# Router logits with the weights held and x streamed, expert choice behind the placing tables, first gate gathered in two rounded parts

## Chip, cores and metric

One core of a Trainium2 chip. The metric is the device time of one execution in microseconds (us); three runs of the kernel before give the median, and one more execution was profiled.

## What is computed

Two transformer stacks in a row on 256 tokens of width 1024, all in float32. In the first stack each of two layers ends in a mixture of experts, the part that the change touches (the reference, cut):

```python
def hier_moe(x, w_group, b_group, w_router, b_router, w_gate, w_up, w_down):
    t = x.reshape(-1, D)
    g_logits = (t @ w_group) + b_group                    # 4 groups
    g_prob = softmax(g_logits); g_idx = argmax(g_logits)
    g_w = g_prob at g_idx
    e_logits = ((t @ w_router).reshape(-1, 4, 4) + b_router) at g_idx
    top_w, top_i = top_k(softmax(e_logits), 2)
    top_w = top_w / sum(top_w)
    combine = onehot(g_idx) * within(top_i, top_w) * g_w  # 16 weights a token
    for e in range(16):
        y += combine[:, e] * ((silu(t @ w_gate[e]) * (t @ w_up[e])) @ w_down[e])
```

A token goes to one group of four experts. The second stack (dense feed-forward layers and a mixer) is left as it is.

## The kernel before, in words

The program of each engine is written out in order, and the engines meet at semaphores; nothing reorders it. TensorE works in rounded float32 (f32r). A value is split in two rounded parts, a high one (ScalarE, a rounding copy) and a low one (VectorE, value minus high part), and a product is three matmuls: high by high, high by low, low by high (L447 to L449). Weights come in units of 128 x 2048, 1 MB. SyncE loads unit i once TensorE has used unit i - 7, ScalarE rounds it (L404) once unit i - 4 is used, VectorE makes the low part (L416). In layer 0, GpSimd does that for one of the units.

The 256 tokens are two tiles (t = 0, 1). In a layer's mixture of experts the tokens are sorted by group: matrices of zeros and ones, `Pm`, put up to 128 tokens of a group in a row (`place_dve`, L1450), and TensorE gathers x by them, two groups at a time (`gather_two_pe`, L1261). The very first gate product, of expert 0, is computed for all 256 tokens while the routing is being worked out, and its result is gathered afterwards (`first_gate_pe`, L1330). All other experts work on gathered tokens, one tile of 128: gate, SiLU on ScalarE (L1527), times up and the token's weight on VectorE (L1535, the hidden block `hd`), turned by TensorE (L1544), down, and back to the tokens' places by `PT`, the turned `Pm` (`place_turn_pe`, L1457 and L1460).

The routing stage runs once a layer. TensorE (`route_pe`): logits of tile 0 (24 matmuls, x held as weights, 20 router columns streamed, L1296), gate unit 0 for tile 0, turning of x of tile 1 (L558), gate unit 1 for tile 0, logits of tile 1, gate unit 0 for tile 1, ranks of the tokens in their groups (L1308 to L1312), gate unit 1 for tile 1; then the gather of groups 0 and 1, the gather of the first gate's product, and the turning of `Pm` for group 0. Then come up units 2 and 3 (numbered from the first gate unit, 0), with the gather of groups 2 and 3 between them, gate units 4 and 5 of expert 1, with the turning of the first hidden block behind unit 4.

VectorE (`route_dve`): low parts of the turned x (L570) and of x itself (L1248), low part of unit 2, bias addition to the logits (L1386), choice of the group, choice of the two experts, placing tables, the tokens' weights `comb` (L1439), low parts of units 3 and 4, of the gathered x (L1279), tables of groups 2 and 3, units 5 and 6, the second gather, the hidden block. ScalarE (`route_act`): high parts of the turned x (L566), of units 2 and 3 (L404), of x (L1244), two exponentials, unit 4, SiLU of the first gate's two tiles (L1358), high parts of the gather (L1272). GpSimd scales X into Y (L1567) once `comb` is there.

## Time and profile before

| | us |
|---|---|
| median of 3 runs | 1907.75 (1907.04 to 1908.02) |
| profiled execution, its own time | 1906.78 |
| its span in the profile | 1905.0 |
| TensorE busy | 1860.3 |
| VectorE busy | 1295.7 |
| ScalarE busy | 1006.0 |

The span is what the rows below count in: us from its start. TensorE's mean granted clock is 0.986 of full speed. A matmul of an f32 tile without rounding shows as two records, one of f32r as one; in both the output's type is what the profile prints.

### The profile page before, as it was taken

Reading aid. Unit: us, or ns where it says so; the run is one execution under the profiler, and the core shown is the slowest. Engines: PE = TensorE matmul, PEld = TensorE weight load, DVE = VectorE, ACT = ScalarE, POOL = GpSimd, SP = SyncE. Lnnn points to the kernel's source line nnn. Section 1 sums busy time; section 2 is a strip of 40 time slices with the busy share of each in tenths; the row PEclk is TensorE's granted clock in tenths of the full one; section 3 lists DMA queues with packets and bytes.
Section 4 is the critical chain, followed back from the end, with each engine's and each line's share of the span. In section 5 each row is a group of like instructions: output and inputs, shape, how many; then the busy total and the mean of one; then the engine's idle time right before and its main releaser. Section 6 shows DMA issues by size and latency. Waiting matters only on the chain.

```text
span 1905.0 us, 21839 instructions
## 1 busy us (share of the span) xinstructions
PE 1860.3 (98%) x9118; PEld 1549.1 (81%) x9118; DVE 1295.7 (68%) x1313; ACT 1006.0 (53%) x1069; POOL 123.5 (6%) x105
## 2 busy tenths in 40 slices
PE   7999999998999999998999999999999999999998
PEld 6788888887978888886888887888888888778886
DVE  4569999997778898997555657655464545676544
ACT  6446777774646777774443364444344424635431
POOL 1021000001011000000000300100010003020000
PEclk9999999999999999998999999999999998999999
DMA  9447999996435999996555642655565556336551
GB/s 339 152 147 249 358 370 359 357 361 201 145 129 196 370 356 358 357 372 213 179 196 172 214 138 88 202 194 169 188 221 178 177 175 206 120 131 201 184 178 59
DMA packets 220170, 426.56 MB, mean 224 GB/s; under 512 B 7560, under 2 KB 28304, under 8 KB 220064
## 3 DMA queue, kind: packets, MB, share of 16 engines
q1 hardware_dynamic: 214256, 406.91, 62.0%
q0 software_dynamic: 5808, 18.17, 3.0%
q8 instruction: 74, 1.21, 0.3%
q14 instruction: 32, 0.26, 0.0%
HBM read 423.99 MB, written 1.06 MB: 223 GB/s over the span
## 4 chain that ended last, share of the span: by engine, by line
PE 92%; DVE 4%; ACT 2%; DMA 1%; issue 1%; POOL 0%; DVEq 0%; SPq 0%
PE ps L447 26%; PE ps L449 26%; PE ps L448 26%; DVE Wlo L416 2%; PE ps L558 2%; PE ps L2429 1%; PE ps L2399 1%; PE ps L2335 1%; ACT Whi L404 1%; PE ps L1544 1%; PE ps L538 1%; PE ps L537 1%; PE ps L536 1%; PE ps L2415 1%; PE ps L1937 1%
## 5 line engine op out<-in xcount | busy, mean ns | idle before, releaser
L416 DVE TENSOR_TENSOR Wlo<-raw,Whi 128x2048 fp32r<-128x2048 f32 (+2 forms) x387 | 868.3, 2247 | 445.1 <-ACT Whi L404 444.4
L404 ACT ACTIVATE Whi<-raw 128x2048 fp32r<-128x2048 f32 (+2 forms) x393 | 736.3, 1877 | 480.6 <-PE ps L449 476.1
L447 PE MATMUL ps<-Whi,XTh 128*128 128x512 f32 (+2 forms) x1504 | 579.3, 385 | 14.2 <-DVE Wlo L416 8.1
L449 PE MATMUL ps<-Whi,XTl 128*128 128x512 f32 (+2 forms) x1504 | 569.7, 379 | 0.0
L448 PE MATMUL ps<-Wlo,XTh 128*128 128x512 f32 (+2 forms) x1504 | 569.4, 379 | 0.0
L447 PEld LDWEIGHTS ps<-Whi,XTh 128*128 128x128 f32 x1504 | 287.6, 191 | 70.7 <-DVE Wlo L416 9.6
L449 PEld LDWEIGHTS ps<-Whi,XTl 128*128 128x128 f32 x1504 | 286.8, 191 | 52.5
L448 PEld LDWEIGHTS ps<-Wlo,XTh 128*128 128x128 f32 x1504 | 287.4, 191 | 49.8 <-issue 0.5
L447 PE MATMUL ps<-Whi,hTh 128*128 128x512 f32 x352 | 137.7, 391 | 0.0
L449 PE MATMUL ps<-Whi,hTl 128*128 128x512 f32 x352 | 137.1, 389 | 0.0
L448 PE MATMUL ps<-Wlo,hTh 128*128 128x512 f32 x352 | 137.0, 389 | 0.0
L447 PE MATMUL ps<-Whi,mo_hTh 128*128 128x512 f32 x256 | 100.9, 394 | 0.0
L447 PE MATMUL ps<-Whi,XGh 128*128 128x512 f32 x256 | 100.8, 394 | 0.0
L664 POOL TENSOR_TENSOR rs<-rs,cst 128x1 f32<-128x1 f32 x20 | 30.6, 1528 | 1073.7 <-DVE rs L656 1073.7
L449 PE MATMUL ps<-Whi,mo_hTl 128*128 128x512 f32 x256 | 99.8, 390 | 0.0
L449 PE MATMUL ps<-Whi,XGl 128*128 128x512 f32 x256 | 99.8, 390 | 0.0
L448 PE MATMUL ps<-Wlo,mo_hTh 128*128 128x512 f32 x256 | 99.7, 389 | 0.0
L448 PE MATMUL ps<-Wlo,XGh 128*128 128x512 f32 x256 | 99.7, 389 | 0.0
L449 PEld LDWEIGHTS ps<-Whi,hTl 128*128 128x128 f32 x352 | 66.1, 188 | 13.9
L447 PEld LDWEIGHTS ps<-Whi,hTh 128*128 128x128 f32 x352 | 66.1, 188 | 13.4
L448 PEld LDWEIGHTS ps<-Wlo,hTh 128*128 128x128 f32 x352 | 66.1, 188 | 13.3
L566 ACT ACTIVATE XTh<-ps 128x512 fp32r<-128x512 f32 (+1 forms) x44 | 23.6, 577 | 97.8 <-PE ps L558 97.6
(327 smaller groups left out, 1867.5 us busy)
## 6 DMA issues: line engine op xcount, KB each, us to landing
raw<-in_moe_w_gate SPq DMA_DIRECT2D x64, 1024.0 KB, 5.4
raw<-in_moe_w_up SPq DMA_DIRECT2D x64, 1024.0 KB, 5.5
raw<-in_moe_w_down SPq DMA_DIRECT2D x64, 1024.0 KB, 5.7
raw<-in_ffn_gate SPq DMA_DIRECT2D x44, 1024.0 KB, 5.1
raw<-in_ffn_up SPq DMA_DIRECT2D x44, 1024.0 KB, 5.1
raw<-in_ffn_down SPq DMA_DIRECT2D x40, 1024.0 KB, 5.0
raw<-in_w_in SPq DMA_DIRECT2D x18, 1024.0 KB, 6.4
raw<-in_a_w_in SPq DMA_DIRECT2D x10, 1024.0 KB, 12.3
```

Of the source, the lines that this page charges most:

```text
L404: act.activation(Whi[:, i % NS, 0:m * n], raw[:, i % NR, 0:m * n], ACT.Copy).then_inc(w_rounded, tick(w_rounded, "rounded", i))
L416: dve.tensor_tensor(Wlo[:, i % NR, 0:m * n], raw[:, i % NR, 0:m * n], h.bitcast(f32), ALU.subtract).then_inc(w_rest, tick(w_rest, "rest", i))
L447: pe.matmul(o, xh(k, t), h[:, q, :], start=k == first, stop=False)
L448: pe.matmul(o, xh(k, t), l[:, q, :], start=False, stop=False)
L449: x = pe.matmul(o, xl(k, t), h[:, q, :], start=False, stop=k == end)
L536: pe.matmul(o, h[:, q, c], XTh[:, q, :], start=q == 0, stop=False)
L537: pe.matmul(o, h[:, q, c], XTl[:, q, :], start=False, stop=False)
L538: x = pe.matmul(o, l[:, q, c], XTh[:, q, :], start=False, stop=q == m - 1)
L558: x = pe.transpose(PS[b][:, q * 128:(q + 1) * 128], blk, cst[:, C_ID:C_ID + 128])
L566: act.activation(dst, src, ACT.Copy).then_inc(act_done, tick(act_done, "hi", *name))
L664: pool.tensor_tensor(rs[:, t, 1:2], rs[:, t, 0:1], cst[:, C_ONE + 1:C_ONE + 2], ALU.pow).then_inc(pool_done, tick(pool_done, "root", v, t))
L1544: x = pe.transpose(PS[b][:, q * 128:(q + 1) * 128], hd[:, u, q * 128:(q + 1) * 128], cst[:, C_ID:C_ID + 128])
```

## The change

The router's weights become the held operand: high and low part side by side, 40 columns (`rws`), and x's high and low parts of a tile are streamed, 128 columns a matmul, 16 matmuls a tile. The result stands turned, 40 x 256. VectorE copies it out of PSUM (`lgT`), and two small full-precision matmuls turn it back and add the two parts by a constant table (`C_SUM`), in the middle of gate unit 0 of tile 1.

TensorE does both gate units of tile 0 and the turning of x ahead of all logits. The product of the first gate is no longer put through SiLU before its gather: it is split in a high and a low part (`fgh`, `fgl`), gathered by four rounded matmuls, and SiLU comes behind. The placing tables are made ahead of the choice of the two experts. The turning of `Pm` for group 0 stands behind up unit 2. The low part of unit 2 moves from ahead of the bias addition to behind the gather's low parts.

```diff
@@ -17,7 +17,8 @@
 C_ALL1 = 1352
 C_IOTA = 1480
 C_OWN = 1608
-C_N = 1616
+C_SUM = 1616
+C_N = 1640
 
 
 def constant_table():
@@ -48,6 +49,7 @@
         t[:, C_CADD + 16 * tt:C_CADD + 16 * tt + 16] = np.where(see, 0.0, NEG)
         t[:, C_CMUL + 16 * tt:C_CMUL + 16 * tt + 16] = see
     t[:, C_OWN:C_OWN + 8] = i[:, None] // 16 == np.arange(8)[None, :]
+    t[:40, C_SUM:C_SUM + 20] = i[:40, None] % 20 == np.arange(20)[None, :]
     t[:, C_I4:C_I4 + 4] = 4 - np.arange(4)[None, :]
     t[:, C_ONE] = 1.0
     t[:, C_ONE + 1] = -0.5
@@ -209,8 +211,7 @@
     lam = small("df_lam", [128, 4, 64])
     gs = small("df_gs", [128, 1])
     rw = small("rw", [128, 8, 20])
-    rwh = small("rwh", [128, 8, 20], f32r)
-    rwl = small("rwl", [128, 8, 20], f32r)
+    rws = small("rws", [128, 8, 2, 20], f32r)
     rb = small("rb", [128, 20])
     lg = small("lg", [128, 2, 20])
     comb = small("comb", [128, 2, 16])
@@ -1221,11 +1222,11 @@
 
     def router_act(act, l):
         act.wait_ge(*on("rw", l))
-        act.activation(rwh[:, :, :], rw[:, :, :], ACT.Copy).then_inc(act_done, tick(act_done, "router_hi", l))
+        act.activation(rws[:, :, 0, :], rw[:, :, :], ACT.Copy).then_inc(act_done, tick(act_done, "router_hi", l))
 
     def router_dve(dve, l):
         dve.wait_ge(*on("router_hi", l))
-        dve.tensor_tensor(rwl[:, :, :], rw[:, :, :], rwh[:, :, :].bitcast(f32), ALU.subtract).then_inc(
+        dve.tensor_tensor(rws[:, :, 1, :], rw[:, :, :], rws[:, :, 0, :].bitcast(f32), ALU.subtract).then_inc(
             dve_done, tick(dve_done, "router", l))
 
 
@@ -1281,25 +1282,34 @@
             free(dve_done, *n)
 
 
+
+
+    lgT = at_("lgT", [40, 256], f32, big_o + 32768)
+
     def route_pe(pe, l, v):
-        b = bank(pe, "logits", l, hold=True)
+        b = bank(pe, "logitsT", l, hold=True)
         name, ready = ("gate", l, 0, 0), x_ready(v)
         js = jobs[name]
         bs = [bank(pe, name, t, hold=True) for t in range(2)]
 
         def logits(t):
-            for g in range(2):
-                pe.wait_ge(*on("lo", "xT", v, t, g))
-            first = True
             for k in range(8):
-                for a, w in ((XTh, rwh), (XTh, rwl), (XTl, rwh)):
-                    x = pe.matmul(PS[b][:, 32 * t:32 * t + 20], a[:, k, t * 128:(t + 1) * 128], w[:, k, :],
-                                  start=first, stop=(k == 7 and a is XTl))
-                    first = False
+                ready(pe, k, t)
+                for a in (XTh, XTl):
+                    x = pe.matmul(PS[b][0:40, t * 128:(t + 1) * 128], rws[:, k].rearrange("p a n -> p (a n)"),
+                                  a[:, k, t * 128:(t + 1) * 128], start=k == 0 and a is XTh, stop=k == 7 and a is XTl)
+            x.then_inc(pe_done, tick(pe_done, "logitsT", l))
+
+        def logits_turn():
+            b = bank(pe, "logits", l)
+            pe.wait_ge(*on("lgT", l))
+            for t in range(2):
+                x = pe.matmul(PS[b][:, 32 * t:32 * t + 20], lgT[:, t * 128:(t + 1) * 128], cst[0:40, C_SUM:C_SUM + 20],
+                              start=True, stop=True)
             x.then_inc(pe_done, tick(pe_done, "logits_mm", l))
 
         def gate(u, t):
-            use_unit(pe, js[u], t, bs[t], xt_h, xt_l, ready, 0, 7)
+            use_unit(pe, js[u], t, bs[t], xt_h, xt_l, ready, 0, 7, 2 if (u, t) == (0, 1) else None, logits_turn)
 
         def ranks():
             b = bank(pe, "ranks", l)
@@ -1312,10 +1322,10 @@
             pe.matmul(PS[b][:, 8:12], a1, oh[:, 1, :], start=False, stop=True).then_inc(
                 pe_done, tick(pe_done, "ranks", l))
         pe.wait_ge(*on("router", l))
+        gate(0, 0)
+        gate(1, 0)
+        second_pe(pe, v)
         logits(0)
-        gate(0, 0)
-        second_pe(pe, v)
-        gate(1, 0)
         logits(1)
         held.discard(b)
         gate(0, 1)
@@ -1323,16 +1333,33 @@
         gate(1, 1)
         held.difference_update(bs)
 
+
+    fgh = at_("fgh", [128, 2, 512], f32r, sh_o)
+    fgl = at_("fgl", [128, 2, 512], f32r, sh_o + 4096)
+
+    def first_half_act(act, l, t):
+        name = ("gate", l, 0, 0)
+        act.wait_ge(*product(name, t))
+        act.activation(fgh[:, t, :], PS[where[name, t]][:, :], ACT.Copy).then_inc(act_done, tick(act_done, "gate_hi", l, t))
+
+    def first_half_dve(dve, l, t):
+        name = ("gate", l, 0, 0)
+        dve.wait_ge(*on("gate_hi", l, t))
+        dve.tensor_tensor(fgl[:, t, :], PS[where[name, t]][:, :], fgh[:, t, :].bitcast(f32), ALU.subtract).then_inc(
+            dve_done, tick(dve_done, "gate_lo", l, t))
+        free(dve_done, name, t)
+
     def first_gate_pe(pe, P, l):
         b = bank(pe, "first", l)
         for t in range(2):
-            pe.wait_ge(*on("silu", l, t))
-            x = pe.matmul(PS[b][:, :], Pm[:, t, 0, :].bitcast(f32), sg[:, t, :], start=t == 0, stop=t == 1)
+            pe.wait_ge(*on("gate_lo", l, t))
+            for a in (fgh, fgl):
+                x = pe.matmul(PS[b][:, :], Pm[:, t, 0, :], a[:, t, :], start=t == 0 and a is fgh, stop=t == 1 and a is fgl)
         x.then_inc(pe_done, tick(pe_done, "first", l))
 
     def first_gate_act(act, P, l):
         act.wait_ge(*on("first", l))
-        act.activation(sg[:, 0, :], PS[where["first", l]][:, :], ACT.Copy).then_inc(
+        act.activation(sg[:, 0, :], PS[where["first", l]][:, :], ACT.Silu).then_inc(
             act_done, tick(act_done, P.name, "sg", 0, 0))
         free(act_done, "first", l)
 
@@ -1348,16 +1375,14 @@
         x_split_act(act, l, v, 0)
         second_act(act, v)
         x_split_act(act, l, v, 1)
+        first_half_act(act, l, 0)
         act.wait_ge(*on("group_gap", l))
         act.activation(ex, ex, ACT.Exp).then_inc(act_done, tick(act_done, "group_exp", l))
+        first_half_act(act, l, 1)
+        gather_two_act(act, l, 0)
         act.wait_ge(*on("top_gap", l))
         act.activation(g_(5), g_(5), ACT.Exp).then_inc(act_done, tick(act_done, "top_exp", l))
         round_units(act, js[0] + NS)
-        for t in range(2):
-            act.wait_ge(*product(name, t))
-            act.activation(sg[:, t, :], PS[where[name, t]][:, :], ACT.Silu).then_inc(
-                act_done, tick(act_done, "silu", l, t))
-            free(act_done, name, t)
 
     def first_max(dve, dst, src, tmp, mx, *name):
         dve.wait_ge(*own(dve_done))
@@ -1374,13 +1399,15 @@
             dve_done, tick(dve_done, *name))
 
     def route_dve(dve, l, v):
+        x_split_dve(dve, l, 0)
         x_turn_dve(dve, v, 1)
-        for t in range(2):
-            x_split_dve(dve, l, t)
-        rest_units(dve, last_unit(v) + NS - 1)
+        first_half_dve(dve, l, 0)
         tmp, ex, el, o1, o2 = (o4[:, i, :, :] for i in range(5))
         L4 = lg[:, :, 0:4]
         OH = oh[:, :, :]
+        dve.wait_ge(*on("logitsT", l))
+        dve.tensor_copy(lgT[:, :], PS[where["logitsT", l]][0:40, 0:256]).then_inc(dve_done, tick(dve_done, "lgT", l))
+        free(dve_done, "logitsT", l)
         dve.wait_ge(*on("logits_mm", l))
         dve.wait_ge(*on("rw", l))
         dve.tensor_tensor(lg[:, :, :],
@@ -1389,6 +1416,21 @@
         free(dve_done, "logits", l)
         first_max(dve, OH, L4, tmp, g_(0), "oh", l)
         dve.tensor_tensor(ex, L4, gb_(0), ALU.subtract).then_inc(dve_done, tick(dve_done, "group_gap", l))
+        x_split_dve(dve, l, 1)
+        dve.wait_ge(*on("ranks", l))
+        dve.tensor_copy(rank[:, :, :], PS[where[("ranks", l)]][:, 0:12].rearrange("p (t g) -> p t g", g=4)
+                        ).then_inc(dve_done, tick(dve_done))
+        free(dve_done, "ranks", l)
+        dve.wait_ge(*own(dve_done))
+        dve.tensor_scalar(gm[:, :, :], rank[:, 0:2, :], float(CAP), None, ALU.is_lt).then_inc(dve_done, tick(dve_done))
+        dve.wait_ge(*own(dve_done))
+        dve.tensor_tensor(gm[:, :, :], gm[:, :, :], oh[:, :, :], ALU.mult).then_inc(dve_done, tick(dve_done))
+        dve.wait_ge(*own(dve_done))
+        for g in range(2):
+            place_dve(dve, MAIN[l], g, rank, gm)
+        dve.tensor_scalar(rest[:, :, :], rank[:, 0:2, :], float(CAP), None, ALU.subtract).then_inc(
+            dve_done, tick(dve_done))
+        dve.tensor_reduce(fmax[:, :], rank[0:1, 2, :], AX.X, ALU.max).then_inc(dve_done, tick(dve_done))
 
         pr = bc(lg[:, 0, 4:5], (20, 2), (4, 4), (1, 4))
         pk = bc(pk_[:, 0, 0:1], (16, 2), (4, 4), (1, 4))
@@ -1406,21 +1448,9 @@
         first_max(dve, o2, ex, tmp, g_(4))
         dve.wait_ge(*own(dve_done))
         dve.tensor_tensor(g_(5), g_(4), g_(3), ALU.subtract).then_inc(dve_done, tick(dve_done, "top_gap", l))
-
-        dve.wait_ge(*on("ranks", l))
...
+        first_half_dve(dve, l, 1)
+        gather_two_dve(dve, l, 0)
+        rest_units(dve, jobs["up", l, 0, 0][0])
 
         dve.wait_ge(*on("top_exp", l))
         dve.scalar_tensor_tensor(g_(6), g_(5), 1.0, g_(2), ALU.add, ALU.mult).then_inc(dve_done, tick(dve_done))
@@ -1438,7 +1468,6 @@
         ohb = bc(oh[:, 0, 0:1], (4, 2), (1, 4), (0, 4))
         dve.tensor_tensor(bc(comb[:, 0, 0:1], (16, 2), (4, 4), (1, 4)), o1b, ohb, ALU.mult).then_inc(
             dve_done, tick(dve_done, "comb", l))
-        rest_units(dve, jobs["gate", l, 0, 0][0] + NS)
 
 
     class Path:
@@ -1574,7 +1603,6 @@
         route_pe(pe, l, v)
         gather_two_pe(pe, l, 0)
         first_gate_pe(pe, P, l)
-        place_turn_pe(pe, P, l, 0)
         for g in range(4):
             par = g % 2
             ps = slice(par * 128, par * 128 + 128)
@@ -1607,6 +1635,7 @@
                                 scatter_halves_pe(pe, P, g - 1, t, hf)
                 for z in job_pe(pe, ("up", l, g, j), xh, xl, ready, 1):
                     if z + g + j == 0:
+                        place_turn_pe(pe, P, l, 0)
                         gather_two_pe(pe, l, 1)
             for hf in range(2):
                 for z in job_pe(pe, ("down", l, g, hf), hh, hl, h_ready, 1, hold=int((g, hf) == (3, 1))):
@@ -1628,9 +1657,7 @@
         P = MAIN[l]
         place = act.soon()
         route_act(act, l, v)
-        gather_two_act(act, l, 0)
         first_gate_act(act, P, l)
-        place_turn_act(act, P, 0)
         round_units(act, jobs["gate", l, 0, 0][1] + NS)
         for g in range(4):
             for j in range(4):
@@ -1643,6 +1670,7 @@
                         h_turn_act(act, P, g, j - 1, mTh[:, 4 * j - 4:4 * j, :])
                 for z in job_act(act, ("up", l, g, j), None, 1):
                     if z + g + j == 0:
+                        place_turn_act(act, P, 0)
                         gather_two_act(act, l, 1)
             for hf in range(2):
                 name = ("down", l, g, hf)
@@ -1668,7 +1696,6 @@
         P = MAIN[l]
         place = dve.soon()
         route_dve(dve, l, v)
-        gather_two_dve(dve, l, 0)
         for g in range(2, 4):
             place_dve(dve, P, g, rank, gm)
         rest_units(dve, jobs["gate", l, 0, 0][1] + NS)
```

The order of VectorE's instructions shows two places. First, from the turned x of tile 1 to the bias addition, layer 0, before (names end in h and l for high and low parts):

```order
L672 SCALAR_TENSOR_TENSOR X<-Y,rs,gb 128x512 x2
L83 BRANCH_PREFETCH_HINT
L570 TENSOR_TENSOR XTl<-ps,XTh 128x4x128 x2
L1248 TENSOR_TENSOR Xnl<-X,Xnh 128x1024 x2
L416 TENSOR_TENSOR Wlo<-raw,Whi 128x2048
L1386 TENSOR_TENSOR lg<-ps,rb 128x40
```

and with the change:

```order
L673 SCALAR_TENSOR_TENSOR X<-Y,rs,gb 128x512 x2
L85 BRANCH_PREFETCH_HINT
L1249 TENSOR_TENSOR Xnl<-X,Xnh 128x1024
L571 TENSOR_TENSOR XTl<-ps,XTh 128x4x128 x2
L1348 TENSOR_TENSOR fgl<-ps,fgh 128x512
L1409 COPY lgT<-ps 40x256
L1413 TENSOR_TENSOR lg<-ps,rb 128x40
```

The second half of x's low part and unit 2's low part have left; the first gate's low part and the logits' copy have come.

Second, VectorE from the tokens' weights to the first hidden block, before:

```order
L1439 TENSOR_TENSOR comb<-o_79,oh 128x32
L416 TENSOR_TENSOR Wlo<-raw,Whi 128x2048 x2
L1279 TENSOR_TENSOR XTl<-ps,XTh 128x512 x4
L1450 TENSOR_SCALAR Pm<-cst,rank,gm 128x128 x4
L416 TENSOR_TENSOR Wlo<-raw,Whi 128x2048 x2
L1279 TENSOR_TENSOR XGl<-ps,XGh 128x512 x4
L1535 SCALAR_TENSOR_TENSOR hd<-sg,cwt,ps 128x512
```

and with the change, from the gather's low parts on (the rows left out are the tokens' weights, small ones):

```order
L1280 TENSOR_TENSOR XTl<-ps,XTh 128x512 x4
L417 TENSOR_TENSOR Wlo<-raw,Whi 128x2048
...
L1469 TENSOR_TENSOR comb<-o_78,oh 128x32
L1479 TENSOR_SCALAR Pm<-cst,rank,gm 128x128 x4
L417 TENSOR_TENSOR Wlo<-raw,Whi 128x2048 x4
L1280 TENSOR_TENSOR XGl<-ps,XGh 128x512 x4
L1564 SCALAR_TENSOR_TENSOR hd<-sg,cwt,ps 128x512
```

The gather's low parts have moved ahead of `comb`, with one unit behind them, and four units in a row stand between `comb` and the second gather.

ScalarE in the same stage, before:

```order
L566 ACTIVATE XTh<-ps 128x4x128 x2
L404 ACTIVATE Whi<-raw 128x2048 x2
L1244 ACTIVATE Xnh<-X 128x1024
L1352 ACT_TABLE_LOAD
L1352 ACTIVATE o_79<-o_79 128x8
L1354 ACTIVATE gx<-gx 128x2
```

and with the change:

```order
L567 ACTIVATE XTh<-ps 128x4x128 x2
L405 ACTIVATE Whi<-raw 128x2048 x2
L1245 ACTIVATE Xnh<-X 128x1024
L1343 ACTIVATE fgh<-ps 128x512
L1380 ACT_TABLE_LOAD
L1380 ACTIVATE o_78<-o_78 128x8
```

The first gate's high part, on which VectorE's `fgl` waits, stands behind two units and x.

## Rows read from the trace of the kernel before

**Rows 1.** The page's busy times: us, share of the span, instructions.
```profile
PE 1860.3 (98%) x9118; PEld 1549.1 (81%) x9118; DVE 1295.7 (68%) x1313; ACT 1006.0 (53%) x1069; POOL 123.5 (6%) x105
```

**Rows 2.** Busy us by stage and engine, then granted clock, DMA share, GB/s.
```profile
128.60:133.00 4.40, 4.40 (x14) 3.44 (x14) 2.37 (x3) 0.00 (x0) 2.51 (x3) 0.61 0.45 174
139.20:142.90 3.70, 3.70 (x11) 2.90 (x11) 3.57 (x4) 1.35 (x2) 0.00 (x0) 0.55 0.00 0
240.00:280.00 40.00, 40.00 (x183) 32.93 (x182) 36.06 (x22) 29.93 (x21) 0.00 (x0) 1.00 1.02 366
435.40:439.00 3.60, 3.33 (x7) 1.80 (x8) 2.72 (x5) 0.05 (x1) 0.89 (x1) 0.66 1.10 351
560.70:563.10 2.40, 0.25 (x3) 0.01 (x1) 1.88 (x3) 1.88 (x3) 0.00 (x0) 1.00 1.01 361
```

**Rows 3.** TensorE in order of time, layer 0: start, us, engine, line, operation.
```profile
125.91 0.24 PE L1296 MATMUL ps<-rwh,XTh 128*128 128x20 f32 x1
...
133.01 1.03 PE L558 MATMUL ps<-cst,X 128*128 128x128 f32 x8
...
136.63 0.17 PE L1296 MATMUL ps<-rwh,XTh 128*128 128x20 f32 x1
...
139.22 0.49 PE L447 MATMUL ps<-Whi,XTh 128*128 128x512 f32 x1
...
143.89 0.39 PE L1308 MATMUL ps<-oh,cst 128*128 128x4 f32 x2
...
145.03 0.48 PE L447 MATMUL ps<-Whi,XTh 128*128 128x512 f32 x1
...
148.53 0.38 PE L1261 MATMUL ps<-Pm,Xnh 128*128 128x256 f32 x1 [0.50 <-DVE Pm L1450]
...
152.46 1.88 PE L1330 MATMUL ps<-sg,Pm 128*128 128x512 f32 x4
...
162.27 0.40 PE L447 MATMUL ps<-Whi,XTh 128*128 128x512 f32 x1
...
167.75 0.60 PE L1544 MATMUL ps<-cst,hd 128*128 128x128 f32 x4
...
435.43 0.47 PE L1510 MATMUL ps<-Ygh,PT 128*128 128x512 f32 x1 [3.70 <-DVE Ygl L1698]
```

**Rows 4.** VectorE in order of time, the same stretch.
```profile
130.09 1.42 DVE L672 SCALAR_TENSOR_TENSOR X<-Y,rs,gb 128x512 f32<-128x512 f32 x2 [0.53 <-POOL rs L664]
...
139.30 1.23 DVE L1248 TENSOR_TENSOR Xnl<-X,Xnh 128x1024 fp32r<-128x1024 f32 x1 [2.60 <-ACT Xnh L1244]
...
140.44 2.28 DVE L416 TENSOR_TENSOR Wlo<-raw,Whi 128x2048 fp32r<-128x2048 f32 x1
...
142.65 0.19 DVE L1386 TENSOR_TENSOR lg<-ps,rb 128x40 f32<-128x40 f32 x1
...
149.52 5.33 DVE L416 TENSOR_TENSOR Wlo<-raw,Whi 128x2048 fp32r<-128x2048 f32 x2
...
162.86 2.48 DVE L1279 TENSOR_TENSOR XGl<-ps,XGh 128x512 fp32r<-128x512 f32 x4
...
165.25 0.73 DVE L1535 SCALAR_TENSOR_TENSOR hd<-sg,cwt,ps 128x512 f32<-128x512 f32 x1
```

**Rows 5.** ScalarE in order of time, the same stretch.
```profile
133.64 1.09 ACT L566 ACTIVATE XTh<-ps 128x512 fp32r<-128x512 f32 x2 [8.66 <-PE ps L558]
...
138.21 1.05 ACT L1244 ACTIVATE Xnh<-X 128x1024 fp32r<-128x1024 f32 x1
```

**Rows 6.** TensorE in order of time, full-precision matmuls of 128 columns.
```profile
1140.32 1.05 PE L2433 MATMUL ps<-mx_wcT,mx_vcz 128*128 128x128 f32 x8
```

**Rows 7.** GpSimd in order of time, the scaling of X.
```profile
149.70 7.78 POOL L1567 TENSOR_SCALAR Y<-X 128x1024 f32<-128x1024 f32 x2 [16.77 <-DVE comb L1439]
```

**Rows 8.** Tile lg: ns min/median/max, first and last start us.
```profile
L1386 DVE TENSOR_TENSOR lg<-ps,rb x2: 191/192/193, 142.6 to 579.9; 128x40 f32<-128x40 f32 x2
```

**Rows 9.** Line 518: weight loads of 16 columns, ns.
```profile
L518 PEld LDWEIGHTS ps<-XTh,Whi x8: 93/94/95, 21.3 to 23.8; 128*16 128x16 f32 x8
```

13 lines of the change are left out of this document (removed).

## The prediction

> **What bounds the kernel now.** I read the page's busy shares first. TensorE is busy for 1860.3 of 1905.0 us, VectorE for 68% [rows 1]: time is won where TensorE idles, repeats or runs slowly, and lost where another engine makes it wait. Then the busy times by stage: inside the experts' loop TensorE works 40.00 of 40.00 us at the full clock [rows 2], so whatever the routing stage before it gains or loses stays to the end. Third, TensorE in order of time through the routing stage of layer 0, from the first router matmul at 125.91 us to the first turn of a hidden block at 167.75 us [rows 3]. Layer 1 repeats it 437.2 us later: the addition of the router's bias starts at 142.6 and 579.9 us [rows 8]. The change touches only this stage, so I work out one pass, and take it twice.
>
> The stage costs more than its arithmetic. One token tile's logits are 24 matmuls of 20 moving columns: 2.59 us (136.63 to 139.22) [rows 3]. Behind each such block the granted clock falls: 0.61 over 128.6 to 133.0 us, 0.55 over 139.2 to 142.9 us, so most of these stretches ran at 1.2 GHz instead of 2.4 [rows 2]. A weight unit takes 2.74 us at the full clock (162.27 to 167.75 is two); the one from 139.22 took until 143.89, 4.67 us [rows 3]. Last I read VectorE and ScalarE over the same stretch [rows 4, 5], since the change reorders them more than it does TensorE.
>
> **The change, part by part.** A unit is 1 MB of weights; gate units 0 and 1 are the first expert's, up units 2 and 3 follow, then 4, 5 and 6.
>
> *TensorE up to the logits.* New order: both gate units of tile 0, the turning of tile 1, both logits, gate unit 0 of tile 1. From 125.91 us: two units, 5.5 us, to 131.4; the turn 0.8 us (133.01 to 136.63 is 3.6 with a unit in it) [rows 3], to 132.2; X of tile 1 is complete at 130.09 + 1.42 = 131.5 us [rows 4]. The logits are now 2 x 16 matmuls, 40 weight columns, 128 moving columns of rounded type. No row has that form. Lower bound: 0.11 us each, the pace of the present ones (2.59 / 24), or less, since the weights are narrower. Upper bound: 0.22 us, two records of 128 full-precision columns (8 records in 1.05 us; with the last one's own end of about 0.25 taken off they start 0.11 apart, two to a matmul) [rows 6]. I take 0.22, the only row with 128 moving columns, and keep the lower one as a rival. So 7.0 us, to 139.2. Half a unit, 1.4 us, to 140.6. Two small full-precision matmuls turn the logits back: four records at the pace of the rank matmuls (10 in 143.89 to 145.03), 0.45 us. The bias addition can start at 141.2 us; before, 142.65 [rows 4]. Lead: 1.4 us. With 7.0 us of wide matmuls for 5.2 us of narrow ones I expect no fall of the clock here, which is worth some 1.7 us per block (4.67 or, from the first, about 4.4 against 2.74).
>
> The Trainium skill, page "TensorE: Matmul & The Clock Gate", section "LDWEIGHTS (loading the stationary operand)", has the load time go with the number of columns; the trace agrees in direction, 94 ns for 16 columns [rows 9] against a mean of 170 over all loads (1549.1 / 9118) [rows 1]. With its 56 ns of section "Back-to-back issue gap" for 128 columns the 32 matmuls would take an estimated 1.8 us; that falls in the first rival.
>
> *A new wait ahead of the logits' copy.* VectorE now computes the low part of the first gate's tile 0 before it copies the logits out. For that it needs ScalarE's high part, which stands behind two roundings and the rounding of X. From the first turned copy to the end of that X rounding is 133.64 to 139.27, 5.6 us [rows 5]. With the turn at 131.4 ScalarE starts at 132.0 (0.63 behind it, as now) and is through at 137.7; the high part, a 128x512 copy of about 0.55 us, at 138.2; VectorE's low part, 0.62 (a quarter of 2.48 [rows 4]), at 138.9; the copy of the logits about 0.4 more, 139.3. TensorE wants it at 140.6: hidden by 1.3 us if a logits matmul costs 0.22, a stall if it costs 0.11 or less.
>
> *VectorE from the bias addition to the first hidden block.* Before: 142.65 to 165.98 us, 23.3 us [rows 4]. To this the change adds: the low part of unit 2, 2.2 us, which stood ahead of the addition (140.44 to 142.65); the low part of X's tile 1, 1.1 us (139.30 to 140.44); tile 1 of the first gate's low part, 0.6 us. Both the logits and the hidden block now enclose them. Three units instead of two are subtracted while GpSimd scales X for 7.78 us [rows 7]; the two there took 5.33, so 2.67 each, against 2.28 for one alone [rows 4]: 0.4 us. And two short waits, for the ranks and for the last quarter of the gather, about 0.5 us. Sum 4.8 us. The hidden block ends at 141.2 + 23.3 + 4.8 = 169.3 us. It ended at 165.98, and TensorE took it at 167.75: it was 1.6 us early, not counting 0.2 us from the end to the start of the next. Now it is taken at 169.5.
>
> *TensorE behind the logits.* 141.05 + 1.4 + ranks 1.1 + unit 2.8 = 146.4: the gather starts 2.1 us before today's 148.53, and its matrices are ready. Gather 3.9 (148.53 to 152.46) [rows 3], to 150.3. The first gate's gather, four rounded matmuls of 0.23 instead of full precision, about 0.95 for 1.7 us, to 151.3. Then up unit 2 needs its low part, which VectorE now makes behind the gather's: at about 154.2. TensorE idles 3 us. Up unit 2.8, placing turn 0.7 (moved here), second gather 3.8, two units 5.5: 167.0. The turn of the hidden block waits until 169.5, 2.5 us. Before: 167.75. **Net: 1.7 us later, per layer, 3.4 us in all.** What TensorE itself gained, 3.6 us per layer, goes into two waits for VectorE. Behind it VectorE catches up, since it is busy for 36.06 of 40 us in the loop [rows 2], and the DMA queue is paced by TensorE's use of buffers, so it shifts as a whole.
>
> The sum stands against the profiled execution, 1906.78 us: 1910.2. The median of the three runs is 1.0 us above it, 1907.75: **1911.2 us**, 0.18% more. Some 0.2%, 3.8 us, is what a measurement of this kernel can tell from no change.
>
> **The rivals.**
> *The logits matmuls cost 0.11 us or less* (20 in 100). TensorE then wants the copy at 137.2 or earlier, and stalls to 139.3: the bias addition starts at 140.1, 1.1 us earlier than forecast. The rest is VectorE's chain: +0.6 us per layer, 1909.0 us. For it: the present rounded matmuls show no sign of more than one pass.
> *VectorE's chain does not decide* (16 in 100). If its 4.8 us were 1 us or less, or the work between overlapped more than I see, TensorE alone sets the pace: 151.3 + 2.8 + 0.7 + 3.8 + 5.5 = 164.1 against 167.75, 3.6 us gained per layer: 1900.5 us. Half of it would give 1904. Against it: the order of VectorE's instructions is fixed, and all of them stand before the hidden block.
> *The clock falls behind the new waits* (14 in 100, the side of slower). TensorE idles 3 us before up unit 2 and 2.5 us before the hidden block's turn. A fall behind the first is covered by the second wait; a fall behind the second costs 1.7 us per layer, as measured behind the logits. 1914.6 us, or 1912.9 if it comes in one layer. It decides once the second wait is long enough to lower the clock. For it: behind a present wait, in which TensorE did nothing until 435.43 us, the granted clock is 0.66 over the next 3.6 us [rows 2, 3]. Against it: that wait lasts 3.70 us; over the one at 560.7 to 563.1 us, 2.4 us and thus the length of the second, the clock stays at 1.00 [rows 2]. [...]
> *The change does little of what it says* (5 in 100): the clock still falls in the stage, since the two small matmuls and the ranks remain narrow. It would cost up to 1.7 us per layer before the gather, half covered by the wait for up unit 2: 1912 to 1913.
>
> **How the numbers follow.** The forecast itself has 45 in 100, with a range of its own from 1909.5 to 1913. The range of all runs from 1904.5, which takes in half of the gain without the waits, to 1914.6. Slower by over 0.2% (above 1911.6): the clock's rival, the last one, and a third of the forecast: 0.34. Faster by over 0.2% (below 1903.9): most of the second rival: 0.15. The rest, 0.51, is within 0.2%.
>
> **What would show it.** Right, if TensorE's first hidden turn begins about 1.7 us later than today, with a wait for VectorE of some 2.5 us before it, and one of some 3 us before the first up unit. A logits matmul should start every 0.22 us, and the granted clock between 126 and 143 us be full. The gather should start near 146.4 us, and the logits' copy wait for nothing but the logits. Wrong, if the hidden block is taken without a wait, or if VectorE's stretch from the bias addition to it is nearer 23 than 28 us.

## The result and the profile after

The changed kernel takes **1915.97 us** (median of 19 runs, 1908.96 to 1922.55) against 1908.15 us (19 runs, 1906.66 to 1912.01) for the kernel before: ratio 1.0038, 95% interval 1.0030 to 1.0047, slower by 0.38%. I had forecast 1911.2 us with a range to 1914.6, so the direction of the likeliest number was right and its size was not: some 8 us were lost, not 3.4, and the median lies above the range.

The page's busy times of the changed kernel, the row that answers to [rows 1]:

```profile
PE 1857.3 (97%) x9094; PEld 1546.3 (81%) x9094; DVE 1298.5 (68%) x1319; ACT 1006.7 (53%) x1069; POOL 134.1 (7%) x105
```

TensorE works 3.0 us less than before and the span is 9.3 us longer (1914.3 against 1905.0), so it idles 57.0 us where it idled 44.7. The clock is slower as well: the mean granted clock is 0.984, before 0.986. The stretches at half speed in the trace add up to 61.3 us of the span, against 51.9, and 9.4 us more of them cost up to 4.7 us. So up to half of the loss is the clock, which the forecast had booked as a gain, and the rest is waits that outweigh the work saved. Busy time by stage (PE, PEld, DVE, ACT, POOL, then granted clock, DMA share, GB/s), the routing stage of layer 0 in the first three rows, a stretch of the experts, and the routing stage of layer 1 in the rest:

```profile
125.90:138.90 13.00, 10.23 (x71) 8.32 (x70) 8.10 (x13) 6.82 (x7) 5.23 (x4) 1.00 0.57 197
139.60:143.00 3.40, 3.40 (x12) 2.78 (x11) 2.23 (x8) 0.21 (x1) 0.00 (x0) 0.50 0.00 0
143.00:168.90 25.90, 21.69 (x131) 18.77 (x131) 23.95 (x51) 16.35 (x19) 13.09 (x2) 1.00 0.48 162
240.00:280.00 40.00, 40.00 (x184) 33.08 (x183) 36.31 (x22) 30.24 (x22) 0.00 (x0) 1.00 1.03 368
566.30:569.70 3.40, 3.40 (x10) 2.66 (x9) 3.11 (x6) 0.00 (x0) 1.30 (x1) 0.50 0.33 129
579.90:590.10 10.20, 9.18 (x28) 7.85 (x29) 6.18 (x27) 0.21 (x1) 0.00 (x0) 0.50 0.32 104
```

The experts' stretch reads as before [rows 2]: TensorE busy throughout at the full clock. Most of the loss is in the routing stage. Up to 138.9 us layer 0 no longer has the first slow stretch of [rows 2]. The second one is still there, at half clock (1.2 GHz) over 139.6 to 143.0 us, and in layer 1 the clock is at half over 579.9 to 590.1 us, three times as long, and once more at the stage's opening.

TensorE in order of time, layer 0, the answer to [rows 3]:

```profile
132.41 0.22 PE L1299 MATMUL ps<-XTh,rws 128*40 128x128 f32 x1
...
133.20 0.22 PE L1299 MATMUL ps<-XTl,rws 128*40 128x128 f32 x1
...
134.49 0.22 PE L1299 MATMUL ps<-XTl,rws 128*40 128x128 f32 x1
139.28 0.78 PE L1307 MATMUL ps<-cst,lgT 40*128 40x20 f32 x4 [3.13 <-DVE lgT L1409]
142.71 0.42 PE L1318 MATMUL ps<-oh,cst 128*128 128x4 f32 x2
146.72 0.28 PE L1262 MATMUL ps<-Pm,Xnh 128*128 128x256 f32 x1
150.57 0.40 PE L1357 MATMUL ps<-fgh,Pm 128*128 128x512 f32 x1
154.34 0.50 PE L448 MATMUL ps<-Whi,XTh 128*128 128x512 f32 x1 [2.68 <-DVE Wlo L417]
168.95 0.66 PE L1573 MATMUL ps<-cst,hd 128*128 128x128 f32 x4 [1.58 <-DVE hd L1564]
```

Three waits for VectorE stand there where [rows 3] has one of 0.50: 3.13 us for the turned logits' copy, 2.68 for the low part of up unit 2, 1.58 for the hidden block. The first one I had called hidden. The logits are the reason: from the third to the sixteenth matmul of tile 0, 132.41 to 133.20 us, 13 steps take 0.79 us, **0.061 us a step**, where I had taken 0.22. TensorE therefore stands at the copy well ahead of VectorE. (The Trainium skill, page "TensorE: Matmul & The Clock Gate", section "Wait — 56ns, not 53.3ns?", gives 55.6 ns a step for 128 columns at the full clock; this trace comes near it, at 61 for rounded float32.)

VectorE and ScalarE in the same stretch, the answers to [rows 4, 5]:

```profile
132.69 1.29 DVE L571 TENSOR_TENSOR XTl<-ps,XTh 128x512 fp32r<-128x512 f32 x2
138.21 0.69 DVE L1348 TENSOR_TENSOR fgl<-ps,fgh 128x512 fp32r<-128x512 f32 x1 [4.23 <-ACT fgh L1343]
138.82 0.41 DVE L1409 COPY lgT<-ps 40x256 f32<-40x256 f32 x1
140.09 0.20 DVE L1413 TENSOR_TENSOR lg<-ps,rb 128x40 f32<-128x40 f32 x1 [0.87 <-PE ps L1307]
144.06 0.17 DVE L1421 COPY rank<-ps 128x12 f32<-128x12 f32 x1 [1.57 <-PE ps L1322]
...
155.21 1.83 DVE L1479 TENSOR_SCALAR Pm<-cst,rank,gm 128x128 fp32r<-128x128 f32 x4
156.96 8.88 DVE L417 TENSOR_TENSOR Wlo<-raw,Whi 128x2048 fp32r<-128x2048 f32 x4
...
168.16 0.73 DVE L1564 SCALAR_TENSOR_TENSOR hd<-sg,cwt,ps 128x512 f32<-128x512 f32 x1
```

```profile
133.03 3.72 ACT L405 ACTIVATE Whi<-raw 128x2048 fp32r<-128x2048 f32 x2
136.64 1.05 ACT L1245 ACTIVATE Xnh<-X 128x1024 fp32r<-128x1024 f32 x1
137.58 0.60 ACT L1343 ACTIVATE fgh<-ps 128x512 fp32r<-128x512 f32 x1
```

This is the chain of the new wait. The copy of the logits (`lgT`) stands behind `fgl` on VectorE; `fgl` needs `fgh`; `fgh` stands behind two weight units and x on ScalarE. VectorE itself does nothing for 4.23 us ahead of it, with the logits lying in PSUM (the memory that TensorE writes its results to) from about 134.7 us on.

Layer 1 repeats the pattern, and there it costs far more:

```profile
565.90 0.51 PE L448 MATMUL ps<-Whi,XTh 128*128 128x512 f32 x1 [2.17 <-DVE Y L680]
...
580.92 1.04 PE L1307 MATMUL ps<-cst,lgT 40*128 40x20 f32 x4 [3.14 <-DVE lgT L1409]
...
584.62 0.42 PE L1318 MATMUL ps<-oh,cst 128*128 128x4 f32 x2
```

From the wait's end to the ranks is 3.43 us in layer 0 (139.28 to 142.71) and 3.70 us here; but the clock stays at half for another 5.5 us behind the ranks' start. The first row above shows a wait of 2.17 us for `Y`, at the start of layer 1's stage. In a table, between points that both traces have (waits are those in front of the point):

| stretch | before | after | difference |
|---|---|---|---|
| layer 0, first gate work to first hidden turn | 125.9 to 167.75 | 125.9 to 168.95 | +1.20 |
| to the wait for Ygl at the end of its experts | to 435.43 | to 437.35 | +0.72 |
| to the start of layer 1's routing stage | to 563.12 | to 565.90 | +0.86 |
| layer 1, to its first hidden turn | to 605.01 | to 613.29 | **+5.50** |
| to the wait for Ygl at the end of its experts | to 871.95 | to 880.23 | 0.00 |
| the rest | to 1905.0 | to 1914.3 | +1.02 |

The same instructions cost 1.20 us in one layer and 5.50 in the other. The work and the waits are alike (3.13 and 3.14, 2.68 and 2.68, 1.58 and 1.62 us); what differs is 10.2 us at half clock against 3.4 in the wait's wake. 6.8 us more at half speed are up to 3.4 us of time, and the stage's opening has 3.4 us of it as well (566.3 to 569.7), up to 1.7 us more.

The table's other rows hold 2.60 us that lie outside the two stages. There the clock is at half over 436.6 to 443.4 us and over 880.3 to 894.0 us, 6.8 and 13.7 us long, where the trace of before has 3.4 us (from 436.5) and 10.2 us (from 873.5). That is up to 1.7 us more each time, in places that the change does not touch.

### The profile page after: what moved, and what is told of

Its sections match the earlier page's. It is cut to its first block, busy times and chain, and to the rows that moved or that the text cites. A ratio compares the mean times of both kernels' runs of the same rounds, so it can differ in the third digit from the quotient of the medians.

```text
span 1914.3 us, 21795 instructions
## 1 busy us (share of the span) xinstructions
PE 1857.3 (97%) x9094; PEld 1546.3 (81%) x9094; DVE 1298.5 (68%) x1319; ACT 1006.7 (53%) x1069; POOL 134.1 (7%) x105
## 4 chain that ended last, share of the span: by engine, by line
PE 92%; DVE 4%; ACT 2%; DMA 1%; issue 1%; POOL 0%; DVEq 0%; SPq 0%
PE ps L448 26%; PE ps L450 26%; PE ps L449 26%; DVE Wlo L417 2%; PE ps L559 2%; PE ps L2456 1%; PE ps L2426 1%; ACT Whi L405 1%; PE ps L2362 1%; PE ps L1573 1%; PE ps L539 1%; PE ps L538 1%; PE ps L537 1%; PE ps L2442 1%; PE ps L1964 1%
```

## The experiments

Two theories at first. **The clock**: the long wait for the turned logits makes the granted clock fall, and that fall, not the wait, is the main loss. **The chain**: VectorE's longer way to the hidden block is the loss, as in my forecast, and the clock only accompanies it. The kernels ran in three groups, each beside runs of the kernel before on the same chip (medians 1907.8, 1907.2 and 1908.1 us). The changed kernel itself was measured beside other runs of the kernel before (1908.15 us), so between it and an experiment the ratios, each to its own runs of before, are safer than the medians.

**1. The logits' copy ahead of the first gate's low part** (takes the wait away).

```diff
     def route_dve(dve, l, v):
         x_split_dve(dve, l, 0)
         x_turn_dve(dve, v, 1)
-        first_half_dve(dve, l, 0)
...
         dve.tensor_tensor(ex, L4, gb_(0), ALU.subtract).then_inc(dve_done, tick(dve_done, "group_gap", l))
+        first_half_dve(dve, l, 0)
         x_split_dve(dve, l, 1)
```

> The changed kernel, with VectorE's copy of the turned logits (lgT) ahead of the first gate's low part instead of behind it. In the changed kernel TensorE waits 3.13 us for that copy (layer 0), and the granted clock falls right behind. Theory (the loss is the wait for the copy with the fall of the clock behind it, plus VectorE's longer chain): the 3.1 us wait goes, no fall of the clock near the ranks, the bias addition starts near 136.6 us instead of 140.09, and the turn of the first hidden block begins near 165.5 us instead of 168.95; time about 3 us under the kernel before, so some 10 us under the change. Rival (only VectorE's chain from the bias addition to the hidden block counts, the clock does not): 3.5 us per layer gained against the change's layer 0, so the same in layer 0, but the two layers gain equally. Rival (the loss sits elsewhere, behind the routing stage): less than 2 us gained.

Measured 1904.91 us (1902.51 to 1911.78), ratio to before 0.9984 (0.9975 to 0.9993): against the changed kernel's 1.0038 some 10 us won by moving one instruction of 0.69 us. TensorE in layer 0:

```profile
135.76 0.62 PE L1307 MATMUL ps<-cst,lgT 40*128 40x20 f32 x4
...
149.89 0.79 PE L448 MATMUL ps<-Whi,XTh 128*128 128x512 f32 x1 [2.68 <-DVE Wlo L417]
165.53 0.60 PE L1573 MATMUL ps<-cst,hd 128*128 128x128 f32 x4
```

The logits are turned 3.5 us earlier, without a wait, and the hidden block is taken at 165.53, 3.4 us earlier. Now the wait for unit 2 is the long one, and the clock is at half for 6.8 us from 149.2 us on, 0.7 us before that wait ends. Layer 1's stage (561.94 to 602.54 us) takes 40.60 us instead of 47.39, so the layers do not gain equally, as the rival without the clock wanted. But the mean granted clock is hardly better than the changed kernel's, 0.985 against 0.984, worth up to 1.7 us: most of this gain is the wait that is gone and all that now starts earlier.

**2. The wait filled** (keeps it, takes TensorE's idleness away): 14 matmuls of 512 columns, whose result is overwritten.

```diff
         def logits_turn():
             b = bank(pe, "logits", l)
+            for q in range(14):
+                pe.matmul(PS[b][:, :], XTh[:, q % 8, 128:256], halves(js[0])[0][:, q % 4, :], start=True, stop=True)
             pe.wait_ge(*on("lgT", l))
```

> The changed kernel with 14 matmuls of 512 columns put in TensorE's wait for the turned logits; they write a bank that is written anew afterwards and change no result. The wait itself stays as it is, TensorE is only busy in it. Theory (the clock falls because of this wait and costs several us, more in layer 1): the half-clock stretch behind it vanishes in both layers, the time falls from about 1916 to 1909 to 1911 us, and the spread between runs shrinks to that of the kernel before. Rival (the clock's part is small, the loss is the chain of waits): within 1 us of the change or slower by it, since 3 us of work were added to a wait of 3.1.

Measured 1906.37 us (1905.58 to 1909.97), ratio 0.9994 (0.9985 to 1.0003), 9.6 us below the changed kernel by the medians and 8.4 by the ratios, more than the expected 5 to 7.

```profile
135.84 3.36 PE L1306 MATMUL ps<-Whi,XTh 128*128 128x512 f32 x14
139.13 0.62 PE L1309 MATMUL ps<-cst,lgT 40*128 40x20 f32 x4
```

```profile
139.60:143.00 3.40, 3.40 (x22) 2.93 (x22) 2.74 (x11) 0.21 (x1) 0.00 (x0) 1.00 0.13 23
577.00:590.00 13.00, 10.32 (x65) 8.99 (x65) 11.84 (x42) 6.40 (x10) 0.00 (x0) 0.99 0.50 163
152.80:156.20 3.40, 3.40 (x9) 2.62 (x10) 3.30 (x11) 2.46 (x3) 2.49 (x1) 0.50 0.01 2
589.70:593.10 3.40, 3.35 (x8) 2.71 (x9) 3.26 (x12) 2.66 (x3) 2.31 (x1) 0.50 0.01 2
```

So the clock is a large part of the loss. The turned logits come hardly earlier than in the changed kernel (139.13 against 139.28), the order of VectorE's work is untouched, TensorE has 3.2 us more work per layer, and the kernel is 0.4 to 0.5% faster. The clock is at 1.00 and 0.99 where it was at 0.50. The first hidden turns are at 167.27 and 604.36 us, against 168.95 and 613.29: layer 1's stage, from 562.73 us, takes 41.63 us instead of 47.39.

It does not isolate one fall, though. In each layer 3.4 us at half clock have moved to the wait for unit 2 (the last two rows), where the changed kernel's layer 0 has 1.00. The mean granted clock is 0.988, and the stretches at half speed add up to 44.9 us against the changed kernel's 61.3. Nearly 7 of these 16 us are the stretches behind the logits (3.4 and 10.2 us) less the two new ones; the others are gone from 436, 566 and 880 us, which the filling does not touch. Why those change is open.

**3. Half the filling.**

```diff
-            for q in range(14):
+            for q in range(7):
```

> The changed kernel with 7 matmuls of 512 columns (1.6 us) in the 3.1 us wait for the turned logits, half of what the filled kernel has, so that TensorE is idle for some 1.5 us. If an idle stretch of that length leaves the granted clock alone, this is the filled kernel again: median 1906.4, first hidden turns at 167.3 and about 604.4 us. If the narrow matmuls of the logits have their part in the fall as much as the idle time, the clock falls as in the changed kernel: half speed for 3.4 us in layer 0 and 10.2 us in layer 1, median 1914 to 1916. Between them, with 3.4 us in each layer, about 1909 to 1911.

Measured 1910.01 us (1905.93 to 1917.31), ratio 1.0011 (0.9998 to 1.0025). The profiled execution met the first case: waits of 1.51 and 1.53 us for the logits, granted clock 1.00 and 0.98 behind them, hidden turns at 167.06 and 604.21 us. But the twelve runs do not lie together: five are at 1905.9 to 1906.7 with a mean clock of 0.988, the other seven between 1908.4 and 1917.3, and those above 1911 have 0.982 to 0.986. The trace shows that an idle stretch of 1.5 us can leave the clock alone. The slower runs had a lower clock somewhere, but whether behind this wait is not shown: none of them was traced.

**4. The low part of unit 2 early**, in VectorE's own idle stretch ahead of `fgl` (takes work out of the chain, keeps the wait for the logits).

```diff
         x_turn_dve(dve, v, 1)
+        rest_units(dve, jobs["up", l, 0, 0][0])
         first_half_dve(dve, l, 0)
...
-        rest_units(dve, jobs["up", l, 0, 0][0])
```

> The changed kernel with the low part of unit 2 in VectorE's idle stretch ahead of the first gate's low part (it waits 4.2 us there for ScalarE), instead of behind the first gather. Theory: the wait for the copy and its clock stay as in the change; TensorE's wait of 2.68 us before the first up unit goes, VectorE's chain to the first hidden block is 2.2 us shorter, and that block's turn begins near 166.9 us in layer 0 instead of 168.95, so 2 us per layer and 4 us in all below the change, about 1912. Rival (the waits behind the gather are covered by others): under 1 us.

Measured 1912.75 us (1910.14 to 1913.74), ratio 1.0021 (1.0012 to 1.0030). The hidden turn comes at 166.98 us, 2.0 earlier, as the chain's sum wants it:

```profile
139.47 0.62 PE L1307 MATMUL ps<-cst,lgT 40*128 40x20 f32 x4 [3.13 <-DVE lgT L1410]
166.98 0.83 PE L1573 MATMUL ps<-cst,hd 128*128 128x128 f32 x4 [2.29 <-DVE hd L1564]
```

The 2.68 us wait is gone and the last one has grown to 2.29. So the chain is real: unit 2's place in it is worth 3.2 us in the median. The clock is now at half for 3.4 us behind the hidden block's wait as well (from 167.3 us), and in layer 1 for 10.2 us at the logits' wait, as in the changed kernel.

**5. Both reorderings**, those of 1 and 4 together, with unit 2's low part directly behind the logits' copy.

> Both: the logits' copy first, then unit 2's low part, and the first gate's low part behind the choice of the group. Theory: no wait for the copy, no wait for the first up unit, the first hidden block's turn near 163 us in layer 0, against 167.75 before and 168.95 with the change; about 4.5 us per layer under the kernel before, 1898 to 1901 us. If the clock is not what makes layer 1 worse, layer 1 gains 4 us less than this against the kernel before.

Measured 1900.40 us (1898.48 to 1905.30), ratio 0.9961 (0.9950 to 0.9973). The hidden turn comes at 163.54 us, with the wait of 2.29 us ahead of it. The gains add: 0.0054 for the first reordering and 0.0017 for the second, against the changed kernel, give 0.0071; together they have 0.0077.

**6. The streamed logits alone**, put into the kernel before, nothing else moved. The diff is the parts of the change that concern `rws`, `C_SUM`, `lgT` and `logits_turn`, and on VectorE

```diff
         x_turn_dve(dve, v, 1)
-        for t in range(2):
-            x_split_dve(dve, l, t)
+        x_split_dve(dve, l, 0)
+        dve.wait_ge(*on("logitsT", l))
+        dve.tensor_copy(lgT[:, :], PS[where["logitsT", l]][0:40, 0:256]).then_inc(dve_done, tick(dve_done, "lgT", l))
+        free(dve_done, "logitsT", l)
+        x_split_dve(dve, l, 1)
```

> The kernel before with the streamed logits alone (weights held, copy of the turned logits, turning back); every other order is that of before, with the copy between the two halves of x's low part on VectorE. Theory, VectorE sets the stage: TensorE is through the two blocks of logits in 1 us each and meets no fall of the clock behind them, but X of tile 1 comes at 131.5 us as before and VectorE still makes the low parts of x and of unit 2 ahead of the bias addition, so this addition moves only with ScalarE, from 142.65 to about 141.0 us; TensorE waits some 2.5 us for the group choice (oh) ahead of the ranks. Hidden turn at about 166 us, median 1904. Rival, the clock falls behind this new wait: the gate unit behind the ranks takes up to 1.7 us more, hidden turn at about 167.7, median 1907 to 1909.

Measured 1906.49 us (1906.00 to 1908.71), ratio 0.9994 (0.9985 to 1.0003). TensorE in order of time, then busy times and clock:

```profile
141.81 0.39 PE L1316 MATMUL ps<-oh,cst 128*128 128x4 f32 x2 [2.50 <-DVE oh L1381]
167.25 0.60 PE L1555 MATMUL ps<-cst,hd 128*128 128x128 f32 x4
```

```profile
142.60:149.40 6.80, 6.80 (x21) 5.64 (x22) 6.22 (x29) 4.37 (x5) 1.79 (x1) 0.51 0.16 60
579.50:586.30 6.80, 6.80 (x21) 5.71 (x22) 6.15 (x31) 3.88 (x4) 1.34 (x1) 0.51 0.23 87
```

The rival's mechanism came in, at a time between the theory's 1904 us and the rival's 1907 to 1909. The logits cost what they should, both old falls of the clock behind them are gone (128.6 to 133.0 and 139.2 to 142.9 in [rows 2]), and the ranks start 2.1 us earlier (143.89 in [rows 3]). But VectorE cannot choose the group sooner, TensorE idles 2.50 us, and the clock falls for 6.8 us behind it: of the 2.1 us, 0.5 is left at the hidden turn. The mean granted clock of the whole kernel is 0.986, as before. The cheaper logits need VectorE's reordering to pay, and it is there that the change loses them.

**7. The first gate in two rounded parts alone**, put into the kernel before. The diff is the change's `first_half_act`, `first_half_dve` and `first_gate_pe`; both low parts are made right behind `comb`.

> The kernel before with the first gate gathered in two rounded parts alone; the low parts are made on VectorE right behind comb. Theory: the gather of the first gate takes 0.95 us instead of 1.7, and VectorE's two low parts (1.3 us) put the hidden block off by 1.3 to 1.4 us, to 167.3, so the hidden turn stays at 167.0 to 167.5 us instead of 167.75: median 1906.5 to 1907.8, no difference that can be measured. Rival: VectorE's idle time absorbs them and the whole 0.75 us per layer is won: 1906.3.

Measured 1914.91 us (1911.08 to 1917.18), ratio 1.0032 (1.0021 to 1.0044). Both expectations missed by 7 us. TensorE does gather the first gate in 0.93 us (from 152.65 to the next work at 153.58) for the 1.88 busy of [rows 3], but

```profile
157.00 0.58 PE L447 MATMUL ps<-Whi,XTh 128*128 128x512 f32 x1 [2.69 <-DVE XTl L1279]
```

```profile
149.73 1.28 DVE L1337 TENSOR_TENSOR fgl<-ps,fgh 128x512 fp32r<-128x512 f32 x2
150.93 5.33 DVE L416 TENSOR_TENSOR Wlo<-raw,Whi 128x2048 fp32r<-128x2048 f32 x2
156.17 2.47 DVE L1279 TENSOR_TENSOR XTl<-ps,XTh 128x512 fp32r<-128x512 f32 x4
```

```profile
157.40:160.80 3.40, 3.40 (x10) 2.69 (x9) 3.40 (x8) 0.10 (x1) 0.00 (x0) 0.53 0.00 0
601.10:604.50 3.40, 3.40 (x9) 2.68 (x10) 3.40 (x8) 0.35 (x1) 0.00 (x0) 0.52 0.00 0
```

Before, the first up unit waited 0.69 us for the gathered x's low parts. TensorE is now faster by 0.9 us and VectorE later by 1.3, so the wait is 2.69, and the clock falls behind it in both layers. I had looked at the hidden block alone, the second meeting point, and not at the nearer one. The hidden turn is at 170.71 us, not 167.5. That is not the whole loss: the profiled execution, at 1917.18 us the slowest of the seven, takes some 3 us more in layer 0's stage and 6 in layer 1's, where the clock is at half for 10.2 us from 566.8 us on, and the trace of before has 3.4.

**8. Both reorderings, and the last low part ahead of the hidden block (unit 6) behind it.** An attempt at the remaining wait of 2.29 us.

```diff
+                if g + j == 0:
+                    gather_two_dve(dve, l, 1)
+                    up(0, where[(name, 0)])
+                    rest_units(dve, jobs[name][-1] + NS)
-                for z in job_dve(dve, name, up, 1):
-                    if z + g + j == 0:
-                        gather_two_dve(dve, l, 1)
+                for z in job_dve(dve, name, up, 1) if g + j else ():
+                    pass
```

> The kernel with both reorderings (logits' copy first, rest of unit 2 early) and the fourth low part behind comb, unit 6, moved behind the second gather's low parts and the hidden block. Theory: the wait for the hidden block (2.29 us) goes, since VectorE reaches it 2.2 us sooner; hidden turn at about 161.4 us in layer 0 (163.54 without this edit), and the clock no longer falls behind it, which is worth up to 1.7 us more per layer: median 1893 to 1896. Rival: unit 6 is late in its turn, or the clock has no part in it: 1896 to 1900.

Measured 1898.44 us (1896.16 to 1900.35), ratio 0.9950 (0.9936 to 0.9965). The order and the clock of the stage are as expected:

```profile
150.96 6.68 DVE L417 TENSOR_TENSOR Wlo<-raw,Whi 128x2048 fp32r<-128x2048 f32 x3
...
159.96 0.73 DVE L1564 SCALAR_TENSOR_TENSOR hd<-sg,cwt,ps 128x512 f32<-128x512 f32 x1
160.62 2.28 DVE L417 TENSOR_TENSOR Wlo<-raw,Whi 128x2048 fp32r<-128x2048 f32 x1
```

```profile
125.90:160.70 34.80, 34.39 (x214) 29.16 (x212) 32.30 (x71) 22.20 (x26) 16.20 (x6) 1.00 0.51 172
857.00:860.00 3.00, 0.33 (x2) 0.32 (x3) 2.52 (x2) 0.25 (x1) 0.00 (x0) 1.00 1.04 387
860.10:873.80 13.70, 9.44 (x27) 6.96 (x26) 9.89 (x16) 1.20 (x2) 4.20 (x4) 0.51 0.10 36
```

TensorE is busy for 34.39 of 34.80 us at the full clock through the whole routing stage. From the ranks to the hidden turn it takes 22.15 us, against 24.35 without the edit, in both layers. But the median gained 2 us, not 5 to 7, and the interval overlaps that of experiment 5. Part of the gain went into a 0.69 us wait at the second hidden turn (173.01 us) and into half-speed stretches elsewhere, of which the profiled execution has 13.7 us at 860 us (10.2 without the edit) and 13.7 at 1085 us (6.8 without).

**9. Both reorderings, and 8 matmuls in the 2.29 us wait instead.** 
```diff
     def h_turn_pe(pe, P, g, j):
...
+        if P in MAIN and g == 0 and j == 0:
+            i = jobs["gate", MAIN.index(P), 0, 1][1]
+            pe.wait_ge(*on("rest", i))
+            for q in range(8):
+                pe.matmul(PS[b][:, :], XGh[0][:, q, 0:128], halves(i)[0][:, q % 4, :], start=True, stop=True)
         pe.wait_ge(*on(P.name, "hd", g, j))
```

> The kernel with both reorderings, and 8 matmuls of 512 columns (1.8 us at the full clock, their result is overwritten) in the 2.29 us in which TensorE waits for the first hidden block. Clock theory: the hidden turn stays at 163.5 us in layer 0, the granted clock behind it stays at 1.00 instead of falling to half for 3.4 us, 1.7 us won per layer: median about 1897. Rival, the fall behind this wait costs nothing that lasts: 1900.4 or, with the added work, more.

Measured 1900.40 us (1898.17 to 1901.26), ratio 0.9962 (0.9948 to 0.9975), the same as without the filling (0.9961). In the trace the fall behind the wait is gone, and from the hidden turn to the end of the layer's experts takes 268.12 us (162.40 to 430.52) against 269.82 (163.54 to 433.36), the 1.7 us of a 3.4 us stretch at half speed. In the median nothing of it shows. Locally confirmed, and as a gain inconclusive.

**10 and 11. TensorE's other long wait filled**, that for `Ygl` at the end of each layer's experts, in the kernel of experiment 8 and in the kernel before.

```diff
     def scatter_halves_pe(pe, P, g, t, hf):
...
         pe.wait_ge(*on(P.name, "PTs", g))
+        for q in range(13 if (g, t, hf) == (3, 0, 1) and P in MAIN else 0):
+            pe.matmul(PS[b][:, :], PT[:, g, 0:128], Ygh[:, 0:512], start=True, stop=True)
         pe.wait_ge(*on(P.name, "yg", g, hf))
```

> The kernel with both reorderings and the late unit, and 13 matmuls of 512 columns (3.0 us, their result is overwritten) in TensorE's wait for Ygl at the end of each layer's experts (4.19 and 3.06 us). Clock theory: the half-speed stretch of 3.4 us behind the wait at 429.75 us goes, and one of the four such stretches that make the 13.7 us from 860.1 us; 1.7 us each: median 1895 against 1898.4. Rival, the waits for X behind it (3.6 to 4 us at 865) bring the fall all the same and only the first is won: 1896.7; or the work delays what follows: 1898.4 or more.

> The kernel before with the same 13 matmuls in its waits for Ygl (3.70 and 3.06 us). Clock theory: the half-speed stretch of 3.4 us at 436.5 us goes, and one of three at 873.4 us: 1.7 us each, median 1903.8 to 1905.5 against 1907.2. Rival: nothing lasting, 1907.2.

In the kernel of experiment 8: **1895.68 us** (1893.67 to 1899.11), ratio 0.9931 (0.9919 to 0.9944), the fastest here, below both kernels of this case; its gain over experiment 8 was measured on another chip, and the two intervals overlap by a little. In its trace the stretch at half clock from 429.9 us is gone and one of 3.4 us at 557.1 us is new; further on stand 10.2 and 6.8 us where experiment 8 has 13.7 and 13.7. In the kernel before: 1911.45 us (1907.19 to 1916.47), ratio 1.0008 (1.0000 to 1.0017), so if anything slower, where the clock theory wanted 3 us won. In its trace (at 1916.47 us the slowest of its runs) the granted clock is 1.00 over 436.3 to 440.0 us, behind the filled wait, of which 1.27 us were left. The later stretches:

```profile
563.80:574.00 10.20, 10.20 (x37) 8.93 (x38) 4.30 (x8) 0.00 (x0) 2.65 (x3) 0.50 0.41 141
1099.60:1113.30 13.70, 13.70 (x65) 13.70 (x65) 0.00 (x0) 3.97 (x5) 0.00 (x0) 0.50 0.25 87
```

So it is full where it should be, and falls for longer in places that nobody touched: 10.2 us from the first logits of layer 1 on, of which the profile of before has 3.4, and 13.7 us at 1099.6 us for 6.8. So filling a wait keeps the clock there, and does not by itself make the kernel faster.

## Why the prediction was wrong, point by point

*TensorE up to the logits.* **This step failed, and with it the next one, the price of the wait.** "I take 0.22" was the price of a logits matmul by full-precision rows, the only ones with 128 moving columns; it measured 0.061. The lower end, "0.11 us each ... or less", was right, and its rival had 20 in 100. With it the bias addition was to start at 140.1 us; it started at 140.09. So the rival's arithmetic held, and its consequence, "+0.6 us per layer", did not. The 56 ns that the prediction takes from the Trainium skill, page "TensorE: Matmul & The Clock Gate", section "Back-to-back issue gap", is there the gap of matmuls without weight loads in between; in this stream with loads it was 61.

*Where the rival's price failed.* It counted the wait for the logits' copy by VectorE's chain alone, and put what the wait does to the clock at nothing. My clock rival did look at waits, but only at the two later ones, because at 0.22 a matmul the first did not exist. Two possibilities were each priced alone, and it is their product that came: 0.061 us a matmul makes a wait of 3.13 us, and the wait a fall of the clock just ahead of the ranks, which VectorE waits for (1.57 us, `rank`). Experiment 2 shows the size: with this wait filled, 8.4 us less by the ratios, and the whole loss is 7.3 (9.6 and 7.8 by the medians). That sum holds the stretches that went from other places, too. By the traces, the clock is up to 4.7 us of the loss against the kernel before. The last rival (5 in 100) had the place, a fall ahead of the gather, and blamed the narrow matmuls; its "up to 1.7 us per layer" fits layer 0's 3.4 us at half clock, and layer 1 had 10.2.

*"I expect no fall of the clock here."* Half right. Through the logits of layer 0 the clock is full, 1.00 up to 138.9 us, where before it was 0.61 over 128.6 to 133.0. It falls behind them, at the end of the wait. By the evidence I used against the rival, the wait of 2.4 us at 560.7 that leaves the clock alone, a wait of up to 2.4 us was harmless; experiments 6 and 7 have falls behind 2.50 and 2.69 us, experiment 4 behind 2.29. Even that wait itself, 2.17 us for `Y`, was no evidence. Every trace has it, and in the changed kernel and in experiments 1, 7, 10 and 11 the clock is at half within some 0.5 us of its end (566.3 us behind 565.90 in the changed kernel). On the other side the 2.68 us wait for unit 2 left the clock at 1.00 in the changed kernel's layer 0. So the length of a wait does not by itself tell whether the clock falls; one row of a harmless wait was no bound. The Trainium skill, page "TensorE: Matmul & The Clock Gate", section "HAM oscillation — how this bites in real kernels", describes just this loss, waits that send the next burst of matmuls off at half clock; the trace agrees, and adds here that shorter waits than those in its example can do it, and that the slow stretch may go on for 10.2 us while TensorE is busy for 9.18 of them.

*VectorE's chain.* Right. Forecast 28.1 us from the bias addition to the end of the hidden block (23.3 and 4.8 more), measured 28.8 (140.09 to 168.89), of which 1.57 is the wait for ranks that came late by the clock; with the clock full it is 27.4 (139.79 to 167.21 in experiment 2). With the bias addition at 140.09 us this chain gives layer 0's 1.20 us. Its items differ: the four subtractions beside GpSimd's scaling took 2.22 us each, not 2.67. GpSimd was slowed instead:

```profile
155.39 13.09 POOL L1596 TENSOR_SCALAR Y<-X 128x1024 f32<-128x1024 f32 x2 [22.43 <-DVE comb L1469]
```

against 7.78 [rows 7], and the second four `Pm` took 1.83 for 1.10 us. Nothing waited for the scaling. The hidden turn was forecast at 169.5 us, with a wait of 2.5; it came at 168.95 with 1.58.

*The wait of some 3 us ahead of up unit 2.* Right: 2.68 us in both layers. The gather was to start near 146.4 and started at 146.72, but that is luck. The logits took 2.33 us (132.22 to 134.55) for the 7.0 of the sum, 4.7 less, and the wait of 3.13 us and the gate unit at half clock, 1.3 us longer up to the ranks, ate it up again.

*Twice the layer.* Wrong. Layer 1 cost 5.50 us and layer 0 1.20. I took the layers as copies, which their instructions are; their clock is not. And "it shifts as a whole" put what lies outside the two stages at nothing; it was 2.60 us more.

*"TensorE alone sets the pace"* (16 in 100, 1900.5 us). Not in this change. With both reorderings, once neither the logits' copy nor the low part of up unit 2 is waited for, the time is 1900.4 us. That the numbers agree is chance: VectorE still makes TensorE wait 2.29 us for the hidden block there, and the logits are 4.7 us cheaper per layer than in that sum.

## What to carry to other kernels

Where a change makes TensorE faster, look for the first place at which it now arrives ahead of another engine, and price the wait there twice: its length, and the matmuls behind it at half clock, in this case up to 5 us for a wait of 3. On the waiting path, put the short instruction that TensorE is about to need (a copy of 0.41 us) ahead of one that itself waits for a third engine. A price taken from the only row of the same width but another precision is a guess; work the plan through at both ends, since a cheaper instruction can be what opens the wait.

## What the runs showed of the hardware that was not expected

- Rounded matmuls with 40 held and 128 moving columns start every 0.061 us at the full clock; the 24 of before, with 128 held and 20 moving columns, every 0.11 us. Streaming the long side brought a tile's logits from 2.59 us to about 1.
- A stretch at half speed can outlast the wait before it by far, with TensorE busy: the kernel of experiment 11 has 10.2 us of it from 563.8 us with TensorE busy throughout. The same instructions behind the same wait of 3.13 us had 3.4 us of it in layer 0 and 10.2 in layer 1; what makes the difference is open.
- The spread of a kernel's runs goes with the granted clock. The changed kernel's run of 1908.96 us has a mean granted clock of 0.988, that of 1920.04 us 0.980; over its 19 runs a straight line gives 1.4 us for each 0.001. Even its fastest run is no faster than the median of before.
- A filled wait kept the clock at that place in the trace of each of the five kernels in which it was tried, one of them half filled. By the medians the gain was 9.6 us in one, some 3 in another (on another chip), none in the third, and a loss of 3.4 in the fourth (1.5 by the ratio, and not clear of noise); the half-filled one varied from run to run. Which later stretches fall, and why they change when work far ahead of them is moved, these runs do not say.
- GpSimd's scaling of x took 13.09 us beside four of VectorE's subtractions in a row and 7.78 beside two with other work behind them. The Trainium skill, page "GPSIMD Engine Reference", section "1. Specifications", says that GpSimd's interfaces to SBUF (the on-chip memory of the tiles) are shared with VectorE, with contention when an instruction of VectorE has two inputs there. The trace agrees as to GpSimd, and shows the subtractions at their usual 2.2 us here but at 2.67 in the kernel before.
